# Third-query turns in one run on VectorE, both key groups' turns in one instruction

## What is computed

```python
u = rms_norm(h, ln) @ w_in            # queries of three groups, and a gate
for g, (_, dil) in enumerate(DIL_GROUPS):      # dilations 1, 4, 16
    q = rms_norm(q_all[:, :, g], g_q[g])
    o_g, lse_g = dilated_group_attention(q, k_sh[:, :, g], v_sh[:, :, g], dil, slopes)
wts = jax.nn.softmax(jnp.stack(lses, axis=-1), axis=-1)
o = jnp.einsum('bshge,bshg->bshe', jnp.stack(outs, axis=3), wts)
return h + (o * jax.nn.silu(gate)) @ w_o
```

## Time and profile before

| | us |
|---|---|
| median of 3 runs | 1403.69 |
| the three runs | 1403.6, 1403.69, 1404.28 |
| profiled execution | 1404.01 |
| its span | 1402.2 |
| TensorE busy | 1395.2 |
| VectorE busy | 1046.5 |
| ScalarE busy | 706.6 |

### The profile page before, as it was taken

The page is one execution under the profiler, slowest core; times in us unless marked ns, Lnnn a source line. Parts: engine busy times, 40 slices in busy tenths (PEclk is TensorE's granted clock), DMA queues, the critical chain, the costliest instruction groups (busy, mean ns, idle before and its releaser), DMA issues.

```text
span 1402.2 us, 20187 instructions
## 1 busy us (share of the span) xinstructions
PE 1395.2 (99%) x6648; PEld 1169.4 (83%) x6648; DVE 1046.5 (75%) x1969; ACT 706.6 (50%) x1032; POOL 102.5 (7%) x67
## 2 busy tenths in 40 slices
PE   9999999999999999999999999999999999999999
PEld 6888888888888888888888888888888888888887
DVE  6767767747667868877877877887887788789653
ACT  6555555646544544544544454544454445454442
POOL 0101001000010001000101100101010110010000
PEclk9999999999999999999999999999999999999999
DMA  9653544455556545645654654565556456555544
GB/s 355 232 173 125 166 143 142 147 190 179 183 187 203 191 151 180 205 155 180 182 194 149 197 181 163 183 198 167 166 188 189 159 186 194 160 181 190 171 165 150
DMA packets 71233, 252.49 MB, mean 180 GB/s; under 512 B 7904, under 2 KB 8288, under 8 KB 71136
## 3 DMA queue, kind: packets, MB, share of 16 engines
q1 hardware_dynamic: 70704, 249.95, 54.7%
q10 hardware_dynamic: 432, 1.31, 0.3%
HBM read 249.14 MB, written 2.10 MB: 179 GB/s over the span
## 4 chain that ended last, share of the span: by engine, by line
PE 94%; DVE 2%; issue 2%; ACT 1%; DMA 0%; POOL 0%; SPq 0%; DVEq 0%; POOLq 0%
PE acc L1271 85%; PE turn L1303 1%; PE score L1514 1%; PE pv_bank L1536 1%; PE score L1519 1%; PE pv_bank L1540 1%; DVE qT L1180 1%; PE pv_bank L1315 1%; PE score L1411 1%; PE score L1413 1%; DVE w_lo L794 1%; PE turn L1397 0%; DMA raw<-in_w_in 0%; PE og_bank L1323 0%; POOL rms L426 0%
## 5 line engine op out<-in xcount | busy, mean ns | idle before, releaser
L794 DVE TENSOR_TENSOR w_lo<-raw,w_hi 128x1024 fp32r<-128x1024 f32 x463 | 574.2, 1251 | 205.9 <-ACT w_hi L478 196.9
L478 ACT ACTIVATE w_hi<-raw 128x1024 fp32r<-128x1024 f32 x463 | 482.4, 1050 | 397.2 <-PE acc L1271 386.0
L1271 PE MATMUL acc<-w_hi,xa_hi 128*128 128x512 f32 x956 | 378.7, 396 | 0.6 <-DVE w_lo L794 0.4
L1271 PE MATMUL acc<-w_hi,xa_lo 128*128 128x512 f32 x956 | 372.8, 390 | 0.0
L1271 PE MATMUL acc<-w_lo,xa_hi 128*128 128x512 f32 x956 | 372.2, 389 | 0.0
L1271 PE MATMUL acc<-w_hi,xb_hi 128*128 128x512 f32 (+1 forms) x640 | 249.4, 390 | 0.0
L1271 PE MATMUL acc<-w_hi,xb_lo 128*128 128x512 f32 (+1 forms) x640 | 245.9, 384 | 0.0
L1271 PE MATMUL acc<-w_lo,xb_hi 128*128 128x512 f32 (+1 forms) x640 | 245.5, 384 | 0.0
L1271 PEld LDWEIGHTS acc<-w_hi,xa_lo 128*128 128x128 f32 x956 | 179.4, 188 | 37.9
L1271 PEld LDWEIGHTS acc<-w_hi,xa_hi 128*128 128x128 f32 x956 | 179.6, 188 | 37.5 <-issue 1.3
L1271 PEld LDWEIGHTS acc<-w_lo,xa_hi 128*128 128x128 f32 x956 | 179.7, 188 | 35.3
(11 more groups left out here) (178 smaller groups left out, 1061.4 us busy)
## 6 DMA issues: line engine op xcount, KB each, us to landing
raw<-in_w_b SPq DMA_DIRECT2D x320, 512.0 KB, 3.6
raw<-in_w_out_a SPq DMA_DIRECT2D x32, 512.0 KB, 3.3
raw<-in_w_out_b SPq DMA_DIRECT2D x32, 512.0 KB, 3.3
raw<-in_w_gate SPq DMA_DIRECT2D x30, 512.0 KB, 3.6
raw<-in_w_kv SPq DMA_DIRECT2D x16, 512.0 KB, 4.3
raw<-in_w_in SPq DMA_DIRECT2D x15, 512.0 KB, 6.2
raw<-in_w_q SPq DMA_DIRECT2D x16, 384.0 KB, 3.0
res<-in_x_tok SPq DMA_DIRECT2D x4, 512.0 KB, 7.8
```

The costliest lines, as they stand in the source:

```text
L478: nc.scalar.activation(w[0][:, s, 0:width], raw[:, s, 0:width], ACT.Copy).then_inc(hi_ready, 1)
L794: nc.vector.tensor_tensor(w[1][:, s, 0:width], raw[:, s, 0:width], w[0][:, s, 0:width].bitcast(F32), ALU.subtract).then_inc(lo_ready, 1)
L1271: last = nc.tensor.matmul(out, x(a), y(b), start=start and k == 0, stop=stop and k == 2, **more)
```

## The change

Three things:

- On VectorE, all 16 turns of the third queries follow their scaling at once in round 0. The low half of step 5 (in the last section: of step 4) comes behind them, and round 1 holds no turns.
- On ScalarE, the gain on the third queries moves from round 2 to round 1, ahead of the high half of step 7 (in the last section: ahead of that of step 5).
- One turn of `K01` takes both key groups, 256 columns: the access pattern is built by hand, with the distance between the groups' columns as a stride of its own, so that the swap of the second group fits in. 16 instructions stand for 32. `Q01`, `K2V0` and `Q2GATE` keep their shapes.

```diff
@@ ScalarE, b_attend
-                if s == 2:
+                if s == 1:
                     act.wait_ge(blocked, (i - 1) * 4 + 4)
                     gain_of(qT, 2, q_gain)
@@ VectorE, b_blocks
-                for first, groups, swap in {Q01: [(0, 2, 0)], K01: [(0, 1, 0), (1, 1, 1)], K2V0: [(0, 1, 1)],
-                                            Q2GATE: [(0, 1, 0)]}[f]:
-                    at = (first + 2 * (f in (K2V0, Q2GATE))) * 2 * SEQ
-                    col = QUAD * (a ^ 2 if swap else a)
-                    src = rows[a * QUAD:(a + 1) * QUAD, buf, :, first * 2 * P:(first + groups) * 2 * P]\
-                        .rearrange("p t (u d) -> p t u d", d=P)[:, :, :, b * QUAD:(b + 1) * QUAD]
-                    dst = x[b * QUAD:(b + 1) * QUAD, at:at + groups * 2 * SEQ]\
-                        .rearrange("p (u t d) -> p t u d", t=TILES, d=P)[:, :, :, col:col + QUAD]
-                    last = nc.vector.transpose(dst, src)
-                return last
+                groups = 2 if f in (Q01, K01) else 1
+                at, swapped = (0, 1) if groups == 2 else (2, 2)
+                if f in (Q01, Q2GATE):
+                    swapped = GROUPS
+                cols = [(at + g) * 2 * SEQ + QUAD * (a ^ 2 if at + g >= swapped else a) for g in range(groups)]
+                src = rows[a * QUAD:(a + 1) * QUAD, buf, :, 0:groups * 2 * P]\
+                    .rearrange("p t (g u d) -> p t g u d", u=2, d=P)[:, :, :, :, b * QUAD:(b + 1) * QUAD]
+                to = x[b * QUAD:(b + 1) * QUAD, cols[0]:cols[0] + QUAD]
+                parts = [list(d) for d in to.ap]
+                dst = bass.AP(to.tensor, to.offset, [parts[0], [P, TILES], [cols[-1] - cols[0] or QUAD, groups],
+                                                    [SEQ, 2], [1, QUAD]])
+                return nc.vector.transpose(dst, src)
@@ VectorE, b_attend
-                if s < 2:
-                    for n in range(8 * s, 8 * s + 8):
+                    for n in range(16):
                         last = b_blocks(Q2GATE, 3, n)
-                    if s == 1:
-                        last.then_inc(blocked, 1)
+                    last.then_inc(blocked, 1)
```

## The result

The changed kernel is slower than before, and by more than forecast. Its median is 1411.07 us (1409.05 to 1411.53, 6 runs) beside 1403.74 (1403.51 to 1404.28, 6 runs) for the kernel before: a ratio of 1.0048, 95% interval 1.0035 to 1.0061. Forecast were 1405.7 and a range up to 1406.9. The profiled execution took 1410.85 us, its span is 1409.0, 6.8 more than before.

A forecast was written before the change was run, and what follows sets the result against it. TensorE, busy 1395.2 of 1402.2 us, was taken as the bound. Back edges 1.60, last section 0.39 and key turns 0 gave +2.0: profiled 1404.01 becomes 1406.0, median 1405.7 us, range 1403.1 to 1406.9.

The forecast's parts named there:

- What bounds the kernel, and what there is to win: TensorE bounds; its score waits for the gain at two back edges and the last section, at most 2.2 us to win.
- Key turns: VectorE: 16 wide key turns of 435 ns per pair replace 32 of 288 ns, 7.0 us instead of 9.2.
- Value: 0: The wide key turns' forecast effect on the kernel's time: none, since TensorE does not wait there in any pair.
- Sixteen turns ahead of the low halves: Back edges: score's wait goes, but step 5's low half makes TensorE 1.22 late; +0.80 us each, +1.60 for two.
- sixteen end at 837.74 + 5.04: First back edge, VectorE: sixteen turns start at 837.74 as before, end at 842.78; only then step 5's low half starts.
- A recorded sign of being wrong: Prediction wrong if idle time ahead of VectorE's first low half after the branch is not near 2.4 us.
- The last section: Score wins 1.09 us and a restart, but the later mask makes TensorE's turn wait for the gated output: +0.39 us.
- The rule weighed: VectorE's loop branch: with two held 256-instruction blocks, a body of 453 instead of 485 might lose the 2.41 us gap.
- Rival 4: Slower: a second gap between branch and step 5's low half, 2.4 us more per back edge, 1410.5 us; chance 0.10.
- Rival 1: The gap at the branch goes with the shorter loop body: 1403.7 us; chance 0.14.
- Rivals 2 and 3: Last section keeps its gain, 1404.1 us, chance 0.10; all is gained at back edges and last section, 1401.5, chance 0.06.

The follow-up runs named there:

- e8: Changed kernel with the pair loop written out on VectorE and ScalarE, and in the last section a later gain and low half of step 6: 1401.46 us.
- e1: Kernel before with the wide key turns alone, third queries' turns and gain where they stood: 1406.15 us, ratio 1.0016.
- e2: Kernel before with only the sixteen turns in one run and the earlier gain, key turns narrow: 1406.11 us, ratio 1.0015.
- e5: Changed kernel with two idle semaphore increments on VectorE ahead of the loop, which then begins at 834: 1404.09 us, ratio 1.0003.
- e6: Kernel before with wide key turns only in the two pairs ahead of the loop, plus 8 idle increments; loop begins at 840: 1402.73 us.
- e7: Kernel before, last section alone changed: sixteen turns first, gain left in place, low half of step 6 behind the first mask: 1402.70 us.
- e11: Changed kernel, unaltered, run once more: 1410.37 us, ratio 1.0049.
- e3: Changed kernel with 32 idle semaphore increments on VectorE ahead of the loop, which then begins at 864: 1403.91 us, ratio 1.0001.
- e4: Changed kernel with VectorE's loop over the pairs written out, ScalarE's loop kept: 1403.29 us, ratio 0.9995.
- e9: Changed kernel with VectorE's loop written out and four idle sums ahead of the turns in pairs 2, 4 and 6: 1411.74 us, ratio 1.0057.
- e10: Changed kernel with VectorE's loop written out and two idle sums ahead of the turns in pairs 2, 4 and 6: 1406.02 us.

## Why the prediction was wrong, and where it was right

**What bounds the kernel, and what there is to win: right.** TensorE's waits at three joins were everything. By the chains e8 wins 0.54 + 0.55 + 1.23 = 2.3 us at them, where 2.2 were worked out.

**Key turns: right in themselves, wrong in value.** The wide key turn takes 436 ns, the nearest row said 435. Groups by form, VectorE, 610 to 846 us, changed kernel:

```profile
L1183 DVE STREAM_TRANSPOSE kT<-rows 32x256 f32<-32x256 f32 x32 | 14.0, 436 | 0.7
```

TensorE waits for none of them. But "Value: 0" left out that the 16 instructions fewer in each pair change the place of the loop: e1 puts this part alone at 2.3 us.

**Sixteen turns ahead of the low halves: the step that failed.** Its sum starts from "sixteen end at 837.74 + 5.04", and 837.74 is a start from the trace of before, with the gap where it was. The gap moved behind step 4's low half. There it is fully exposed; ahead of it, 1.4 us of it lay beside the wait for ScalarE (2.41 idle, of which only 1.00 counted against ScalarE's end at 834.84). So step 5 was 2.32 and 2.55 late, not 1.22: 1.1 to 1.3 more per edge. All behind that start held, as e2 shows with 0.86 and 0.90 measured for 0.80. The second part missing is the clock, 1.6 us at one of the two edges, which the working did not have at all. A recorded sign of being wrong came true: the idle time ahead of the first low half behind the branch was 1.44 us, not near 2.4.

The shares, of 6.8 us in the profiled executions: 2.0 as forecast (2 x 0.80 + 0.39), 1.10 + 1.33 = 2.4 for the gap's new place, 1.6 for the clock, 0.7 at the start; the sum is 6.7. Without one another the parts cost 2.3 (e1) and 2.2 (e2), in sum 4.5; together 7.3 in the medians, where the clock's share is over 1.6, since five of eleven executions show a second fall. The gap and the turns add up on the same low half, and only together do they make waits long enough to be followed by the lower clock.

**The last section: right**, 0.39 forecast and 0.36 measured, with the stated cause (mask 3.03 behind the score worked out, 3.04 measured; the turn waits 1.37 where "about 1.3" was said).

**The rule weighed, and the rivals.** The prediction had the gap go or stay; it did neither. The table above shows what decides: bodies that begin at 834, 840 and 864 and end by 1324 have no gap; the body that begins at 832 has one, and so has the one that ends at 1348. So there is a lower bound between 832 and 834 and an upper one between 1324 and 1348, and no run narrows the upper one further. e5 and e6 were forecast so before they ran. The Trainium skill, "Runtime: NRT & Kernel Launch", section "Instruction fetch mechanics", says that a sequencer holds two blocks of 256 instructions and stalls on a taken branch to a target outside them. By that rule, with the bounds of its blocks taken at 833|834 and every 256 further on, the body of before reaches over the end of the held blocks with its last three instructions and that of the changed kernel over their start with its first two, the wait and the low half of step 4; and the traces agree on whether there is a gap in all five placements.

The profile also records the fetches, as transfers of the kind "instruction" on the DMA queue q14, which it does not divide among the engines. The page of the changed kernel and that of e5:

```profile
q14 instruction: 44, 0.36, 0.1%
```

```profile
q14 instruction: 42, 0.34, 0.1%
```

The kernel before, e2, e7 and e11 have 44 as well (e1 has 45), e3 and e6 have 42; e4, e9 and e10, with ScalarE's loop alone, have 36, and e8, with neither loop, 29. The times in the packed traces put the difference at the back edges: around each of the two (for the first, from 828 to 840 us), 3 transfers in e4, e9 and e10, none in e8, 5 in e3, e5 and e6, and 6 in all kernels with a gap. So VectorE's loop brings two fetches at a back edge where there is no gap and three where there is one. That the gap is a fetch is thereby better founded than by its place alone, but two things do not fit the plain rule. The loops without a gap fetch behind the branch too. And the changed kernel's branch goes to a target outside the held blocks, yet its low half started after 1.44 us, with ScalarE's end, and not after 2.41 as before; only then came the gap. Which transfer ends which gap stays open. The same caution holds for the earlier trace rows, from which the prediction read that the earlier loop has no gap: the 2.43 us of idle time there end with ScalarE's work and could hide a fetch of up to that length.

Rival 4 had the right mechanism ("a second gap like the first falls between the branch and the low half of step 5") and 1410.5, near the 1411.07 measured, but for a partly wrong reason: it priced 2.4 more per edge, and the gap replaced the first one rather than joined it, so that 1.1 to 1.3 came from it and the rest from the clock. Against it stood that no row showed two gaps in a row. That was weak: the change demonstrably moved the loop, and no row said anything on where the gap would fall next. Rival 1, the gap gone, would have been right two instructions further on: e5 measured 1404.09, the rival's time was 1403.7. Rivals 2 and 3 did not occur.

**Open.** Why the clock falls behind one wait of over 2 us and not behind another is not settled; between 1.40 and 2.09 us no wait inside the pairs was tried. That some executions had two falls is worked out from their mean clock and time, not seen in a timeline. ScalarE's own gap behind its branch (2.09 us in the changed kernel, before) was removed only together with other things, in e8, and has no price of its own.

## What to carry to other kernels

A loop body's place in an engine's instructions is a part of the kernel's time: after any edit that adds or removes instructions ahead of or in a loop, look for "issue" idle time in the first rows behind each back edge, and treat it as movable. If it matters, shift the loop by a few instructions that do nothing, or write it out, before judging the edit; here two such instructions were worth more than all of the change. And a wait forecast from rows of before holds only as long as the rows that it starts from keep their place.

## What the runs showed of the hardware

- Behind the branch, VectorE's loop body of 453 instructions that begins at VectorE's instruction 832 leaves 1.9 to 2.2 us of idle time after the first low half; at 834, none. A body of 485 has 2.4 us at 864 and none at 840. Around each back edge the profile has 6 instruction transfers on q14 where there is a gap, 5 where there is none.
- TensorE's clock fell from 2.4 to 1.2 GHz behind three of six waits of 2.09 to 2.39 us (after 2.15, 2.23 and 2.39; not after 2.09, 2.16 and 2.22), and came back after 8 or so intervals of 0.427 us, some 1.6 us of loss. Ahead of all six waits TensorE had worked without a pause for 100 us and more. Behind the waits of 0.9 to 1.40 us in these profiles it did not fall.
- A turn's stride pattern has no price of its own: 32x256 in two query groups and 32x256 with a further stride between two key groups take 436 ns each.
